# Calling square root and exponential once ahead of need, and splitting the wait for the first tokens

## The chip, the cores and the metric

The kernel runs on one core of a Trainium2 chip. The metric is the device time of one execution in microseconds; before the change it is 1632.89 us, the median of three runs (1627.72 to 1634.83). Lower is better.

## What is computed

One inference step of a hybrid backbone with two layers, in float32, on 128 context tokens and 256 latent tokens of 1024 channels:

```
for i in range(2):
    h = rms_norm(x, norm_mix[i]) * (1 + sc1) + sh1
    m = hyena_mixer(h) if i == 0 else rglru_mixer(h)
    x = x + g1 * m
    h = rms_norm(x, norm_moe[i]) * (1 + sc2) + sh2
    x = x + g2 * moe_ffn(h)          # 16 experts, top 2 of the best group
y = rms_norm(x, norm_final)

# moe_ffn, for the tokens of expert e:
scores = softmax(h @ router_w)
y = (silu(xblk @ w1[e]) * (xblk @ w3[e])) @ w2[e]
```

There are five norms: norms 0 and 1 in layer 0, norms 2 and 3 in layer 1 (the code calls the index `tag`; odd ones stand before the experts), and the final one.

## The kernel before

Each engine has a program of its own, written out by hand, and semaphores tie them. `PER` holds, for each semaphore, how often it is raised in a layer; `before(name, l)` is the count before layer l, so that a wait can name a place in a layer.

**Norm.** x lies with the channels on the partitions, in eight tiles of 384 tokens. ScalarE squares each tile as VectorE finishes it (`squares`, L519), TensorE sums over channels by a multiplication with ones, and ScalarE takes the root of 96 columns (`norm_root`, L531). VectorE takes the reciprocal, TensorE spreads it over the partitions, VectorE multiplies (L1366), and ScalarE (five tiles, L540) and VectorE (three) modulate.

**Router.** TensorE computes the logits, ScalarE copies them out (L756), and TensorE transposes them. VectorE reduces, finds the maximum and subtracts it (L1683); ScalarE takes the exponential (L759); VectorE picks groups, experts and gates in a long row of small instructions. Meanwhile ScalarE copies the normed tokens out of PSUM (`token_tile`, L752). ScalarE's table of functions is loaded where an instruction needs another one than is loaded (ACT_TABLE_LOAD in the trace, under the line of the instruction); these loads aren't written in the code.

**Experts.** An expert layer takes the 16 experts two at a time, eight rounds of a loop. For a pair, `tokens_of_two` gathers 64 tokens for each expert, transposed, by multiplying the tokens `h` with one-hot matrices `pick`: the channels 0 to 511 into PSUM bank 0, then 512 to 1023 into bank 6 (`TOKEN_BANKS`). ScalarE copies both banks to `xT` (L764 ahead of the loop, L574 in it). For each expert TensorE then multiplies with w1 (channels 0 to 511 first, then the rest), w3 and w2. The gather for the next pair lies in the second half of a round, between the w3 matrix and the w2 matrix of the pair's second expert. Experts with more than 64 tokens get extra passes of 32. Outputs are combined one expert later and added to x by VectorE (L1774).

**Weights.** SyncE loads 2 MB pieces into eight buffers, six pieces an expert. Those of the first expert and two pieces of the second are loaded ahead; the next wait in the queue (L369, L370) until TensorE has given a buffer back.

The copy ahead of the loop and TensorE's wait for it:

```
act.wait_ge(S("xT_mm"), before("xT_mm", l) + 1)
for i, bank in enumerate(TOKEN_BANKS):
    last = a.activation(xT[:, i, :, :], PS[:, bank, :]..., ACT.Copy)
last.then_inc(S("xT"), 1)
...
pe.wait_ge(S("xT"), before("xT", l) + group + 1)
```

Of the kernel before, what the change touches and what calls it, by code (L numbers as in the profile page):

```python
# [12 lines left out]
ACT = mybir.ActivationFunctionType  # L13
AX = mybir.AxisListType.X

P = 128
# [96 lines left out]
class Chain:  # L113
# [5 lines left out]
    def link(self, instruction):  # L119
# [5 lines left out]

PER = dict(sq=8, ss_mm=1, rms=1, rinv=1, rb_mm=1, nrm=8, hT_act=BY_ACT, hT_dve=KD - BY_ACT, ada_mm=12, o_mm=8, x_upd=8,
           rt_mm=3, rt_ev=1, rt_exp=1, rt_max=1, rt_mask=1, tok_mm=6, tok=6, route=1, pick=18, gpick=17,
           xT_mm=8, xT=8, w1_mm=16, w13_mm=16, sig=16, hid=16, gpT_mm=16, gpT=16, hidT_mm=16, hidT=16, w2_mm=16, yo=16,
           c_mm=128, acc_done=128)
def before(name, index):  # L130

    return PER[name] * index
# [100 lines left out]
def program(nc, A, y_prompt, y_sample, new_state):  # L233
    where, (pool, pool_order, pool_count) = plan(), pool_plan()
    with ExitStack() as ctx:
# [5 lines left out]
        def S(name):  # L241
            if name not in sems:
                sems[name] = ctx.enter_context(nc.semaphore(name))
            return sems[name]
# [20 lines left out]
        small = sb("small", [P, 100])  # L265
        PS = ctx.enter_context(nc.psum_tensor("PS", [P, 8, HALF], F32))
# [17 lines left out]
        eps = small[:, 81:82]  # L284
# [46 lines left out]
        xT = cut(hT, 576, 2 * HALF).rearrange("p (i c m) -> p i c m", i=2, m=P)  # L331
        gpT = cut(hT, 1600, N)
        hid = cut(hT, 1984, HALF)
# [153 lines left out]
        def _(act):  # L487
# [27 lines left out]
            def squares(tag, ks, sem=None, value=0):  # L515
                for n, k in enumerate(ks):
                    if sem is not None:
                        act.wait_ge(S(sem), value + n)
                    a.activation(h_ch[:, k, :], xc[:, k, :], ACT.Square).then_inc(S("sq"), 1)  # L519
# [13 lines left out]
            def modulate(tag):  # L533
# [3 lines left out]
                for k in range(BY_ACT):  # L537
# [3 lines left out]
                                           bias=MOD[:, l, 8 * sh + k, s:s + 1], scale=MODA[:, tag, k, s:s + 1])  # L541
                    ins.then_inc(S("hT_act"), 1)

            def norm(tag, sem, value):
                squares(tag, NORM_ORDER[tag], sem, value)
                norm_root(tag)
                modulate(tag)

            def expert_layer(l):
                with act.Fori(0, NE // UNROLL) as group:  # L550
                    for r in range(UNROLL):
                        e = group * UNROLL + r
                        extra = act.value_load(counts_i[0:1, bass.ds(e, 1)], min_val=0, max_val=NX)
                        done = act.value_load(counts_i[0:1, NE:][0:1, bass.ds(e, 1)], min_val=0, max_val=2 * LAYERS * NX)
                        act.wait_ge(S("w1_mm"), before("w1_mm", l) + e + 1)
                        a.activation(hid, PS[:, 2, :], ACT.Sigmoid).then_inc(S("sig"), 1)  # L556
                        with act.If(extra > 0):
                            with act.Fori(0, extra) as j:
                                n = done + j
                                act.wait_ge(S("x_gpT_mm"), n + 1)  # L560
                                a.activation(XgpT, PS[:, 7, 0:N], ACT.Copy).then_inc(S("x_gpT"), 1)
                                act.wait_ge(S("x_xT_mm"), n + 1)
                                a.activation(XxT, PS[:, 1, 0:256].rearrange("p (c m) -> p c m", m=P), ACT.Copy) \
                                    .then_inc(S("x_xT"), 1)
                                act.wait_ge(S("x_w1_mm"), X_BEGUN + n + 1)
                                a.activation(Xhid, PS[:, 4, 0:256], ACT.Sigmoid).then_inc(S("x_sig"), 1)
                                act.wait_ge(S("x_hT_mm"), n + 1)
                                a.activation(XhidT, PS[:, 0, 0:256].rearrange("p (c m) -> p c m", m=P), ACT.Copy) \
                                    .then_inc(S("x_hT"), 1)
                        if r:  # L570
                            with act.If(group < NE // UNROLL - 1):
                                act.wait_ge(S("xT_mm"), before("xT_mm", l) + group + 2)
                                for i, bank in enumerate(TOKEN_BANKS):
                                    last = a.activation(xT[:, i, :, :], PS[:, bank, :].rearrange("p (c m) -> p c m", m=P), ACT.Copy)  # L574
                                last.then_inc(S("xT"), 1)
                        act.wait_ge(S("hidT_mm"), before("hidT_mm", l) + e + 1)
                        a.activation(hidT, PS[:, 2, :].rearrange("p (c m) -> p c m", m=P), ACT.Copy) \  # L577
                            .then_inc(S("hidT"), 1)
                        act.wait_ge(S("gpT_mm"), before("gpT_mm", l) + e + 1)
                        act.wait_ge(S("c_mm"), SPREAD + before("c_mm", l) + 8 * e)  # L580
                        a.activation(gpT, PS[:, 3, 0:N], ACT.Copy).then_inc(S("gpT"), 1)
# [155 lines left out]
            for l in range(LAYERS):  # L737

                if l == 0:
                    mixer0()  # L740
                else:
                    norm(2, "acc_done", ADDED + before("acc_done", l) - 7)
                    mixer1()

                norm(2 * l + 1, "x_upd", 8 * l + 1)
                if l:
                    act.dma_start(nf, A["norm_final"].partition_broadcast(P)).then_inc(S("nf_in"), 16)

                def token_tile(i):
                    act.wait_ge(S("tok_mm"), before("tok_mm", l) + i + 1)  # L750

                    a.activation(h[:, i // 2, i % 2 * HALF:i % 2 * HALF + HALF].rearrange("p (k c) -> p k c", k=4),  # L752
                                 PS[:, 2 + i, :].rearrange("p (c k) -> p k c", k=4), ACT.Copy).then_inc(S("tok"), 1)

                act.wait_ge(S("rt_mm"), before("rt_mm", l) + 1)
                a.activation(pre[:, 0, :], PS[:, 0, 0:N], ACT.Copy).then_inc(S("rt_ev"), 1)  # L756
                token_tile(0)
                act.wait_ge(S("rt_max"), before("rt_max", l) + 1)
                a.activation(rt(0), rt(0), ACT.Exp).then_inc(S("rt_exp"), 1)  # L759
                for i in range(1, 6):  # L760
                    token_tile(i)
                act.wait_ge(S("xT_mm"), before("xT_mm", l) + 1)
                for i, bank in enumerate(TOKEN_BANKS):
                    last = a.activation(xT[:, i, :, :], PS[:, bank, :].rearrange("p (c m) -> p c m", m=P), ACT.Copy)  # L764
                last.then_inc(S("xT"), 1)
                act.wait_ge(S("route"), before("route", l) + 1)
                expert_layer(l)

            for i in range(6):  # L770
                act.wait_ge(S("y_mm"), i + 1)
                a.activation(hT[:, HALF * i:HALF * i + HALF], PS[:, 2 + i, :], ACT.Square, accum_out=sumsq[:, i:i + 1]) \
                    .then_inc(S("y_sq"), 1)
# [13 lines left out]
        def _(pe):  # L787
# [323 lines left out]
            def tokens_of_two():  # L1111
                for i, bank in enumerate(TOKEN_BANKS):
                    for c in range(4):
                        at = HALF * i + P * c
                        for t in range(NT):
                            last = mm(PS[:, bank, P * c:P * c + P], h[:, t, at:at + P], pick[:, t, :], t == 0, t == NT - 1)
                last.then_inc(S("xT_mm"), 1)

            def weight(r, c):
                return ring[:, moe_slot(r, c), :].rearrange("p (k n) -> p k n", k=4)  # L1120
# [1 line left out]
            def expert_layer(l):  # L1122
# [80 lines left out]
                with pe.Fori(0, NE // UNROLL) as group:  # L1203
                    for r in range(UNROLL):
                        e = group * UNROLL + r
                        extra = pe.value_load(counts_i[0:1, bass.ds(e, 1)], min_val=0, max_val=NX)
                        done = pe.value_load(counts_i[0:1, NE:][0:1, bass.ds(e, 1)], min_val=0, max_val=2 * LAYERS * NX)
                        pe.wait_ge(S("xT"), before("xT", l) + group + 1)
                        for b, at, done_sem in ((2, 0, "w1_mm"), (3, 2, "w13_mm")):
                            for k in range(KD):  # L1210
                                half = k // 4
                                c = at + half
                                if k % 4 == 0:
                                    arrived(c, r, group)
                                for g in range(2):
                                    last = mm(PS[m * g:m * g + m, b, :], xT[:, half, k % 4, m * r:m * r + m],
                                              weight(r, c)[:, k % 4, HALF * g:HALF * g + HALF], k == 0, k == KD - 1)
                            last.then_inc(S(done_sem), 1)
# [71 lines left out]
        def _(dve):  # L1290
# [465 lines left out]
            def expert_layer(l):  # L1756
# [64 lines left out]
                with dve.Fori(0, NE // UNROLL) as group:  # L1821
                    for r in range(UNROLL):
# [9 lines left out]
                        ch.link(take(pcols, rankm, e + 2))  # L1832
                        ch.link(v.tensor_scalar(xcols[:, 0:3], xcols[:, 0:3], -float(BASE), None, ALU.add))
                        extra_picks()
                        dve.wait_ge(S("xT_mm"), before("xT_mm", l) + group + 1)
                        one_hot(pick[:, :, BASE * r:BASE * r + BASE], base_iota, pcols, None, BASE, "pick")

                        dve.wait_ge(S("sig"), before("sig", l) + e + 1)
# [99 lines left out]
```

## Time and profile before

| what | value |
|---|---|
| median of three runs | 1632.89 us |
| the profiled execution's own time | 1633.03 us |
| its span, first to last instruction | 1631.2 us |
| TensorE busy | 1519.3 us, 93% of the span |
| VectorE busy | 688.6 us, 42% |
| ScalarE busy | 311.4 us, 19% |
| mean granted clock of TensorE | 0.976 of full speed |
| moved by DMA | 495.70 MB, mean 304 GB/s |

Busy shares are averages over stages with different limits; what ends a wait is read from the stage itself. A granted clock of 1.00 is 2.4 GHz and 0.50 is 1.2 GHz.

### The profile page before, as it was taken

The numbers are of one execution on the slowest core, as the hardware profiler recorded it, in microseconds if no ns is written. First come the engines' busy times: TensorE is split into PE (matmuls) and PEld (weight loads), VectorE is DVE, ScalarE is ACT, GpSimd is POOL, SyncE is SP. The second block draws the span as 40 slices with busy tenths as digits, with TensorE's granted clock in tenths as the row PEclk, the third lists the DMA queues.
The fourth block names the chain that finished last, engine by engine and source line by source line (L and its number), as shares of the span: only waits on it lengthen the run. The fifth ranks groups of instructions, "written<-read, shape, count | busy, mean of one in ns | idle before, by whom it ended". The sixth has DMA issues, their size and how long they took to land.

```text
span 1631.2 us, 22649 instructions
## 1 busy us (share of the span) xinstructions
PE 1519.3 (93%) x8134; PEld 734.2 (45%) x8135; DVE 688.6 (42%) x2059; ACT 311.4 (19%) x521; POOL 0.2 (0%) x4
## 2 busy tenths in 40 slices
PE   6999999997799999999999799897999998999996
PEld 3454555654344444344343455454344434344432
DVE  3334666433334434343343648835143343343344
ACT  4332222131010111010010347513110001011001
POOL 0000000000000000000000000000000000000000
PEclk9999999998999999999999899997999999999998
DMA  9438767750777999999979601524599997999994
GB/s 342 151 104 306 259 258 258 289 236 17 321 298 305 416 426 428 424 426 428 424 324 409 206 1 52 206 103 168 229 421 424 426 429 337 412 428 424 427 428 182
DMA packets 67568, 495.70 MB, mean 304 GB/s; under 512 B 4464, under 2 KB 21120, under 8 KB 28224
## 3 DMA queue, kind: packets, MB, share of 16 engines
q1 hardware_dynamic: 66048, 489.33, 73.5%
q10 hardware_dynamic: 1472, 5.72, 1.1%
q8 instruction: 32, 0.52, 0.1%
q14 instruction: 16, 0.13, 0.0%
HBM read 493.45 MB, written 1.58 MB: 303 GB/s over the span
## 4 chain that ended last, share of the span: by engine, by line
PE 80%; DMA 10%; DVE 5%; ACT 2%; issue 2%; SPq 0%; DVEq 0%; ACTq 0%
PE PS L789 77%; DMA halves<-in_moe_w 9%; PE PS L793 3%; DMA halves<-in_ada_w 1%; DVE xc L1774 1%; DVE halves L1597 0%; DVE misc L1597 0%; DVE halves L1588 0%; DVE halves L1590 0%; DVE halves L1589 0%; ACT hT L540 0%; ACT halves L694 0%; ACT L759 0%; ACT L531 0%; ACT L699 0%
## 5 line engine op out<-in xcount | busy, mean ns | idle before, releaser
L789 PE MATMUL PS<-halves,hT 128*64 128x512 f32 x3072 | 671.5, 595 | 19.7 <-DMA halves<-in_moe_w 16.6
L789 PEld LDWEIGHTS PS<-halves,hT 128*64 128x64 f32 x3072 | 216.8, 137 | 462.3 <-issue 430.2
L1774 DVE SCALAR_TENSOR_TENSOR xc<-PS,MOD,xc 128x128 f32<-128x128 f32 x592 | 196.0, 410 | 92.2 <-PE PS L789 90.8
L789 PE MATMUL PS<-hT,halves 128*128 128x384 f32 x640 | 219.8, 499 | 8.4 <-ACT halves L660 6.5
L789 PEld LDWEIGHTS PS<-hT,halves 128*128 128x128 f32 x640 | 122.0, 194 | 107.3 <-issue 23.9
L789 PE MATMUL PS<-halves 128*128 128x384 f32 (+1 forms) x336 | 118.5, 512 | 0.7 <-ACT pre L607 0.7
L789 PE MATMUL PS<-hT,misc 64*128 64x384 f32 x512 | 105.7, 521 | 4.1 <-DVE xc L1774 2.4
L789 PE MATMUL PS<-stack,h 128*128 128x128 f32 x768 | 96.7, 290 | 12.5 <-issue 5.2
L1841 DVE TENSOR_TENSOR hT<-hT,PS 128x512 f32<-128x512 f32 x32 | 22.0, 688 | 196.4 <-PE PS L789 196.4
L789 PEld LDWEIGHTS PS<-stack,h 128*128 128x128 f32 x768 | 93.7, 204 | 23.7 <-issue 19.5
L556 ACT ACTIVATE hT<-PS 128x512 f32<-128x512 f32 x32 | 19.1, 597 | 384.5 <-PE PS L789 384.5
L789 PEld LDWEIGHTS PS<-halves 128*128 128x128 f32 x336 | 63.4, 190 | 53.9 <-issue 17.1
L1853 DVE COPY misc<-PS 128x512 f32<-128x512 f32 x32 | 22.1, 692 | 142.4 <-PE PS L789 75.2
L1839 DVE TENSOR_TENSOR hT<-hT,PS 128x512 f32<-128x512 f32 x32 | 22.0, 688 | 112.5 <-ACT hT L556 112.5
L789 PEld LDWEIGHTS PS<-hT,misc 64*128 64x128 f32 x512 | 50.4, 190 | 41.6 <-issue 12.3
L577 ACT ACTIVATE hT<-PS 128x512 f32<-128x512 f32 x32 | 19.1, 597 | 178.0 <-PE PS L793 178.0
L574 ACT ACTIVATE hT<-PS 128x512 f32<-128x512 f32 x28 | 15.2, 595 | 184.2 <-PE PS L789 184.2
L1393 DVE SCALAR_TENSOR_TENSOR h<-pre,VT,h 128x127 f32<-128x127 f32 (+1 forms) x80 | 29.6, 412 | 45.8 <-ACT h L611 28.6
L793 PE MATMUL PS<-cst,hT 128*128 128x128 f32 x272 | 42.1, 299 | 5.0 <-DVE xc L1774 4.1
L789 PE MATMUL PS<-halves,cT 128*32 128x512 f32 x384 | 46.0, 598 | 0.7 <-DMA halves<-in_ada_w 0.7
L607 ACT ACTIVATE pre<-PS,VT 128x384 f32<-128x384 f32 x24 | 14.0, 581 | 165.1 <-PE PS L789 165.1
L793 PEld LDWEIGHTS PS<-cst,hT 128*128 128x128 f32 x272 | 33.3, 177 | 25.3 <-issue 18.9
(233 smaller groups left out, 1065.5 us busy)
## 6 DMA issues: line engine op xcount, KB each, us to landing
halves<-in_moe_w SPq DMA_DIRECT2D x192, 2048.0 KB, 17.6
halves<-in_ada_w SPq DMA_DIRECT2D x48, 1024.0 KB, 6.5
halves<-in_hy_w_in SPq DMA_DIRECT2D x12, 1024.0 KB, 5.1
halves<-in_rg_w_in SPq DMA_DIRECT2D x4, 2048.0 KB, 15.8
halves<-in_hy_w_out SPq DMA_DIRECT2D x4, 1024.0 KB, 8.1
halves<-in_rg_w_out SPq DMA_DIRECT2D x2, 2048.0 KB, 10.1
halves<-in_rg_wa SPq DMA_DIRECT2D x1, 2048.0 KB, 13.2
halves<-in_rg_wx SPq DMA_DIRECT2D x1, 2048.0 KB, 15.5
```

Source lines behind the costliest of these rows:

```text
L556: a.activation(hid, PS[:, 2, :], ACT.Sigmoid).then_inc(S("sig"), 1)
L574: last = a.activation(xT[:, i, :, :], PS[:, bank, :].rearrange("p (c m) -> p c m", m=P), ACT.Copy)
L577: a.activation(hidT, PS[:, 2, :].rearrange("p (c m) -> p c m", m=P), ACT.Copy) \
L607: a.activation(pre[:, ct % 2, :], PS[:, ct % 2, 0:N], ACT.Identity, bias=VT[:, 0, HB + ct:HB + ct + 1]).then_inc(S("in_ev0"), 1)
L789: return nc.tensor.matmul(out, lhsT, rhs, start=start, stop=stop)
L793: return nc.tensor.transpose(out, in_, ident[0:n, 0:n])
L1393: last = v.scalar_tensor_tensor(o, i, weight, o, ALU.mult, ALU.add)
L1774: ins = v.scalar_tensor_tensor(xc[:, k, cs], PS[:, bank, cs], MOD[:, l, 8 * G2 + k, s:s + 1], xc[:, k, cs], ALU.mult, ALU.add)
L1839: ch.link(v.tensor_tensor(hid, hid, PS[:, 2, :], ALU.mult))
L1841: v.tensor_tensor(hid, hid, PS[:, 3, :], ALU.mult).then_inc(S("hid"), 1)
L1853: v.tensor_copy(yo, PS[:, 6, :]).then_inc(S("yo"), 1)
```

## The change

A helper `table(function)` is added. It calls a function on the constant `eps`, one column, into an unused column of `small`, so that the table is loaded there. It is called with square root ahead of the squares of norms 1, 2 and 3 and of the final norm, and with exponential after the modulation of norms 1 and 3, ahead of the copy of the logits.

The gather raises its semaphore once for each bank instead of once for both. ScalarE waits for each bank and raises `xT` for each half. TensorE waits for a half of the tokens right before the first w1 matmul that reads it, and only at a pair's first expert. VectorE's wait counts both banks.

```
-           xT_mm=8, xT=8, ...
+           xT_mm=16, xT=16, ...

+            def table(function):
+
+                a.activation(small[:, 99:100], eps, function).then_inc(S("table"), 1)
+
             def norm(tag, sem, value):
+                if tag:
+                    table(ACT.Sqrt)
                 squares(tag, NORM_ORDER[tag], sem, value)
...
                         if r:
                             with act.If(group < NE // UNROLL - 1):
-                                act.wait_ge(S("xT_mm"), before("xT_mm", l) + group + 2)
                                 for i, bank in enumerate(TOKEN_BANKS):
-                                    last = a.activation(xT[:, i, :, :], PS[:, bank, :].rearrange("p (c m) -> p c m", m=P), ACT.Copy)
-                                last.then_inc(S("xT"), 1)
+                                    act.wait_ge(S("xT_mm"), before("xT_mm", l) + 2 * group + i + 3)
+                                    a.activation(xT[:, i, :, :], PS[:, bank, :].rearrange("p (c m) -> p c m", m=P), ACT.Copy) \
+                                        .then_inc(S("xT"), 1)
...
+                table(ACT.Exp)
                 act.wait_ge(S("rt_mm"), before("rt_mm", l) + 1)
                 a.activation(pre[:, 0, :], PS[:, 0, 0:N], ACT.Copy).then_inc(S("rt_ev"), 1)
...
-                act.wait_ge(S("xT_mm"), before("xT_mm", l) + 1)
                 for i, bank in enumerate(TOKEN_BANKS):
-                    last = a.activation(xT[:, i, :, :], PS[:, bank, :].rearrange("p (c m) -> p c m", m=P), ACT.Copy)
-                last.then_inc(S("xT"), 1)
+                    act.wait_ge(S("xT_mm"), before("xT_mm", l) + i + 1)
+                    a.activation(xT[:, i, :, :], PS[:, bank, :].rearrange("p (c m) -> p c m", m=P), ACT.Copy) \
+                        .then_inc(S("xT"), 1)
...
+            table(ACT.Sqrt)
             for i in range(6):
                 act.wait_ge(S("y_mm"), i + 1)
...
                         for t in range(NT):
                             last = mm(PS[:, bank, P * c:P * c + P], h[:, t, at:at + P], pick[:, t, :], t == 0, t == NT - 1)
-                last.then_inc(S("xT_mm"), 1)
+                    last.then_inc(S("xT_mm"), 1)
...
-                        pe.wait_ge(S("xT"), before("xT", l) + group + 1)
                         for b, at, done_sem in ((2, 0, "w1_mm"), (3, 2, "w13_mm")):
                             for k in range(KD):
...
                                 if k % 4 == 0:
+                                    if b == 2 and r == 0:
+                                        pe.wait_ge(S("xT"), before("xT", l) + 2 * group + half + 1)
                                     arrived(c, r, group)
...
-                        dve.wait_ge(S("xT_mm"), before("xT_mm", l) + group + 1)
+                        dve.wait_ge(S("xT_mm"), before("xT_mm", l) + 2 * group + 2)
```

## Rows read from the trace of the kernel before

**Rows 1.** The page: the chain that ended last, by engine.

```profile
PE 80%; DMA 10%; DVE 5%; ACT 2%; issue 2%; SPq 0%; DVEq 0%; ACTq 0%
```

**Rows 2.** Stretches: us, busy of PE, PEld, DVE, ACT, POOL, granted clock, DMA share, GB/s.

```profile
640.00:700.00 60.00, 57.39 (x303) 25.05 (x301) 21.33 (x74) 5.74 (x9) 0.00 (x0) 1.00 1.01 427
...
934.00:938.00 4.00, 4.00 (x7) 2.04 (x7) 3.69 (x13) 3.98 (x8) 0.00 (x0) 0.50 0.01 4
938.00:942.00 4.00, 4.00 (x12) 2.31 (x11) 2.84 (x17) 0.74 (x3) 0.00 (x0) 0.87 0.00 0
```

**Rows 3.** Groups by line, ScalarE: busy us, mean ns, idle before.

```profile
L531 ACT ACT_TABLE_LOAD x3 | 3.8, 1283 | 0.1
```

**Rows 4.** Timeline, norms 1 and 3: start us, us, instruction, idle before and releaser.

```profile
353.02 0.52 ACT L519 ACTIVATE h<-xc 128x384 f32<-128x384 f32 x1 [2.06 <-DVE xc L1665]
354.04 0.34 ACT L531 ACTIVATE rs<-PS,small 128x96 f32<-128x96 f32 x1 [0.49 <-PE PS L789]
...
1112.02 0.52 ACT L519 ACTIVATE h<-xc 128x384 f32<-128x384 f32 x1 [4.64 <-DVE xc L1665]
1112.56 1.28 ACT L531 ACT_TABLE_LOAD   x1
1113.85 0.34 ACT L531 ACTIVATE rs<-PS,small 128x96 f32<-128x96 f32 x1
```

**Rows 5.** The chain in order of time, norm 2: start us, us, what.

```profile
926.65 0.52 ACT h L519
...
928.49 0.35 ACT rs L531
```

**Rows 6.** Timeline, the end: variance and root.

```profile
1622.72 0.17 DVE L1871 TENSOR_SCALAR small<-small 128x3 f32<-128x3 f32 x1
...
1623.80 0.21 ACT L775 ACTIVATE small<-small 128x3 f32<-128x3 f32 x1
```

**Rows 7.** Timeline, ScalarE before norm 2 and before the final norm.

```profile
922.10 5.07 ACT L519 ACTIVATE h<-xc 128x384 f32<-128x384 f32 x8 [9.13 <-DVE xc L1774]
...
1617.98 0.60 ACT L772 ACTIVATE hT<-PS 128x512 f32<-128x512 f32 x1 [14.36 <-PE PS L793]
```

**Rows 8.** Timeline, the router in layer 0 and in layer 1.

```profile
357.11 4.49 ACT L540 ACTIVATE hT<-hT,MOD,MODA 128x128 f32<-128x128 f32 x10 [2.73 <-DVE hT L1366]
...
362.97 0.49 ACT L756 ACTIVATE pre<-PS 128x384 f32<-128x384 f32 x1 [1.37 <-PE PS L789]
...
364.80 0.21 DVE L1683 TENSOR_TENSOR misc<-misc 128x48 f32<-128x48 f32 x1
...
365.46 0.24 ACT L759 ACTIVATE misc<-misc 128x48 f32<-128x48 f32 x1
...
1119.07 2.34 ACT L540 ACTIVATE hT<-hT,MOD,MODA 128x256 f32<-128x256 f32 x5
...
1123.39 0.49 ACT L756 ACTIVATE pre<-PS 128x384 f32<-128x384 f32 x1 [1.99 <-PE PS L789]
...
1125.22 0.21 DVE L1683 TENSOR_TENSOR misc<-misc 128x48 f32<-128x48 f32 x1
...
1125.90 0.24 ACT L759 ACTIVATE misc<-misc 128x48 f32<-128x48 f32 x1
```

**Rows 9.** Timeline, gather, copies and first matrix, layer 0; first matrices, layer 1.

```profile
375.93 7.18 PE L789 MATMUL PS<-stack,h 128*128 128x128 f32 x48 [2.14 <-DVE stack L1766]
...
384.36 12.23 PE L789 MATMUL PS<-halves,hT 128*64 128x512 f32 x55 [1.26 <-ACT hT L764]
...
1145.15 13.96 PE L789 MATMUL PS<-halves,hT 128*64 128x512 f32 x64 [1.25 <-ACT hT L764]
```

**Rows 10.** Line L1207, TensorE's queue at loop entry: ns, first and last start.

```profile
L1207 PEldq SEQ_ASSERT  x1: 18/18/18, 382.8 to 382.8; - x1
```

**Rows 11.** Timeline, TensorE's weight loads behind a branch in the expert loop.

```profile
556.43 0.95 PEld L789 LDWEIGHTS PS<-hT,misc 64*128 64x128 f32 x8 [0.81 <-issue]
```

**Rows 12.** Waits of SyncE's queue, 364 to 415 us: total, times, longest.

```profile
SPq L369 <- PE PS L789: 18.4, 1, 18.4
```

More of the change, by code:

```diff
@@ L127 @@
            rt_mm=3, rt_ev=1, rt_exp=1, rt_max=1, rt_mask=1, tok_mm=6, tok=6, route=1, pick=18, gpick=17,
-           xT_mm=8, xT=8, w1_mm=16, w13_mm=16, sig=16, hid=16, gpT_mm=16, gpT=16, hidT_mm=16, hidT=16, w2_mm=16, yo=16,
+           xT_mm=16, xT=16, w1_mm=16, w13_mm=16, sig=16, hid=16, gpT_mm=16, gpT=16, hidT_mm=16, hidT=16, w2_mm=16, yo=16,
            c_mm=128, acc_done=128)
```

## Prediction

> **What bounds the kernel now.** I read the chain that ended last first. It stands on TensorE for 80% of the span and on weight transfers for 10%; ScalarE holds 2% [rows 1]. So anything that only shortens ScalarE can give little, and only at the places where TensorE stands still for it. Next the stretches: inside an expert layer, once it is under way, the DMA share is 1.01 and TensorE is busy 57.39 of 60 us, so there the weight stream sets the pace [rows 2]. Both changes lie outside those stretches: at the norms, in the router, at the first expert of each layer and at the end. The question is what each place gives and whether it passes through to the end.
>
 The timeline of the roots [rows 4] shows what matters most here: the load doesn't wait for what the root waits for. At norm 3 the last square ends at 1112.02 + 0.52 = 1112.54, the load starts at 1112.56, the root at 1113.85. The load runs while TensorE still sums the squares.
>
> **The change part by part.** *Roots of norms 2 and 3.* From the start of the last square to the root: 1.02 us without a load (354.04 - 353.02), 1.83 with one at norm 3 (1113.85 - 1112.02) [rows 4], 1.84 at norm 2 (928.49 - 926.65) [rows 5]. Hoisting gives 0.82 + 0.81 = 1.63 us, not two full loads. The hoisted load and call (1.29 from load to next instruction [rows 4] and 0.21, the length of a three-column call [rows 6]) stand before squares that wait for VectorE, 9.13 us at norm 2 [rows 7]; at norms 1 and 3 they wait for the residual in the same way. Without that cover each would cost 1.50 us.
>
> *Exponential of the router, twice.* VectorE's subtraction ends at 364.80 + 0.21 = 365.01, the exponential starts at 365.46 behind its load [rows 8]. With 0.02 us for the handoff it could start at 365.03: 0.43 us gained. In layer 1: 1125.45 against 1125.90, 0.45 us. The hoisted call stands ahead of the copy of the logits, and behind that copy are queued the first token tile and, through TensorE's transposes, VectorE's whole routing. In layer 0 modulation ends at 357.11 + 4.49 = 361.60; 1.29 and 0.21 later it is 363.10, and the copy starts at 362.97 now: up to 0.13 late. In layer 1: 1119.07 + 2.34 + 1.50 = 1122.91, before 1123.39, free. Net 0.30 + 0.45 = 0.75 us (bounds 0.7 and 0.9, if the short call overlaps the copy).
>
> The rows put 0.02 us between the square's end and the load, and 1.29 from there to the root [rows 4]. The Trainium skill (ScalarE: Activation LUTs, What ACT_TABLE_LOAD costs) counts 1.28 us for the load and some 1.38 of drain, 2.66 together. By that rule the copy of the logits would be late by about 1.5 and 0.9 us and the whole sum would be an estimated 3.4 us. The rows have no place for a drain after a short wait, so I go by 1.29.
>
> *Final root.* VectorE's variance is ready at 1622.72 + 0.17 = 1622.89; the root starts at 1623.80 [rows 6]. 0.89 us. The load moves into a wait of 14.36 us [rows 7]. Behind the root only the reciprocal, three scalings and the output transfers follow, each started by the one before, so all of it counts.
>
> *Tokens of the first pair, once per layer.* The gather takes 7.18 us from 375.93, to 383.11. Then ScalarE copies both halves, and TensorE starts the first matrix at 384.36 after 1.26 us of idle time (1.25 in layer 1) [rows 9]. Afterwards the first half's copy runs at about 375.93 + 3.59 = 379.5, under the second half of the gather. The second copy takes about half of the 1.26 us and ends near 383.8. It is wanted only after 16 matmul instructions of 13.96 / 64 = 0.218 us, 3.5 us after 383.1, so it is covered. The first matrix can start as the gather ends. What could come up in place of the wait is the loop's entry: reading two counters into registers. It is over at 382.8, before the gather's last matmul [rows 10]. I take 1.2 us per layer, 2.4 in all; upper bound 1.25 each, lower bound 0.4 each, if starting the loop's block costs TensorE what a branch in the expert loop does, 0.81 us put down to issue [rows 11].
>
> *In the loop* the same split costs and gives nothing: the fourteen pairs of copies run under the combines of the previous expert, far ahead of the next first matrix. TensorE, ScalarE and VectorE have the same number of waits or one more, and the wait of VectorE means the same moment. The cover is those combines and the second matrices; without it a group would gain what the first pair does.
>
> *Does it pass through?* The stream of weights starts anew only when expert 0 gives its buffers back: SyncE waits 18.4 us for TensorE there after the router [rows 12]. So the saturated stretch moves with TensorE's start, and in the mixer and the norms no row shows TensorE waiting for a weight. I pass everything on one to one.
>
> Sum: 1.63 + 0.75 + 0.89 + 2.4 = 5.67 us. The profiled execution took 1633.03 us (span 1631.2 and 1.8 around it), 0.14 above the median of the runs, so 1627.4 and, against the median, 1627.2 us: 0.35% faster. That lies within what a measurement of this kernel can tell from no change, about 0.5% or 8.2 us; the three runs alone spread over 7.1.
>
> **Rivals.** *(a) The split gives little*, since the loop's entry takes the place of the wait. For it: this row is from a queue that waited anyway. Against: it ended before the gather [rows 10]. 5.67 - 1.6 = 4.1 us, 1628.8. Chance 0.07.
>
> *(b) The weight stream swallows what lies ahead of an expert layer*, if its stretch is bound from transfers begun before the router. Only norm 2 and the final root remain, 0.82 + 0.89 = 1.7 us: 1631.2. Against it stands the restart [rows 12]. Chance 0.06.
>
> *(c) TensorE's clock falls better.* The dense matmuls behind norm 2 run at a granted 0.50 (1.2 GHz) and come back to 2.4 within the next 4 us [rows 2]; before that TensorE had been mostly idle through the norm. Half of the busy 4.00 and 0.13 of the next 4.00 are lost there, 2.5 us. A shorter idle time ahead of it may save that, and some 1 us elsewhere: 1632.9 - 5.7 - 3.5 = 1623.7. Chance 0.12.
>
> *(d) The clock falls worse: slower than before.* The moved starts bring low clock to stretches that now run at 2.4 GHz. Each costs what norm 2's does, 2.5 us; it decides from 5.67 us on, that is 11.3 us of dense matmuls moved to 1.2 GHz, three such stretches. With four, 1632.9 - 5.7 + 10 = 1637.2. For it: the mean clock is 0.976, so low stretches exist. Against: the idle times only get shorter. Chance 0.04.
>
> *(e) The exponential or root still loads*, because the loads are placed otherwise than I think and the added calls bring loads without taking any away: 5.67 - 3.27 = 2.4 gained, minus nothing where hidden, 1630.5. Chance 0.03.
>
> **How the numbers follow.** The forecast has 0.68. Its own range is 1625 to 1629.5 by the bounds of the terms (4.0 to 6.0 us) and the scatter of a median. (a) and (e) lie in or beside it. For 8 in 10 I reach to (c) below and (b) above: 1622.8 to 1631.8. Faster by over 0.5% means below 1624.7: most of (c) and the forecast's lower tail, 0.14. Slower by over 0.5% is above 1641, only the far part of (d) and a shift between measurements: 0.02. The rest 0.84.
>
> **What would show it.** Load and root: no load between the last square and the root at norms 2 and 3, and 1.0 us between their starts. Router: the exponential right after VectorE's subtraction, the copy of the logits at most 0.15 us later than now after the modulation. First pair: TensorE's first matrix within 0.1 us of the gather's end. End: the root at VectorE's heels. Wrong: if the wait for the first half is replaced by idle time put down to issue, if TensorE waits more for weights in the expert layers by what the earlier start gave, or if the stretches behind the norms have another granted clock; that last would move the total by more than any single term.

## Result and the profile after

The kernel is 4.3% slower, and the forecast of 0.35% faster was wrong.

| | median | lowest to highest | runs |
|---|---|---|---|
| before | 1631.06 us | 1627.72 to 1634.83 | 4 |
| after | 1700.4 us | 1698.77 to 1703.22 | 4 |

The ratio is 1.0431, with a 95% interval of 1.0412 to 1.045. The profiled execution after took 1698.77 us, with a span of 1697.0; before the span was 1631.2.

The page of the changed kernel comes first: span, instruction queue (packets, MB, share of the DMA engines), the chain by engine and the expert matmuls (busy us, mean ns | idle before them, and what ended most of it).

```profile
span 1697.0 us, 22645 instructions
...
q8 instruction: 95, 1.56, 0.4%
...
PE 82%; DMA 6%; issue 6%; DVE 5%; ACT 2%; SPq 0%; DVEq 0%; ACTq 0%
...
L797 PE MATMUL PS<-halves,hT 128*64 128x512 f32 x3072 | 688.1, 606 | 63.6 <-issue 54.0
```

The same of the kernel before:

```profile
q8 instruction: 32, 0.52, 0.1%
...
L789 PE MATMUL PS<-halves,hT 128*64 128x512 f32 x3072 | 671.5, 595 | 19.7 <-DMA halves<-in_moe_w 16.6
```

In the chain, issue rose from 2% to 6% and DMA fell from 10% to 6% [rows 1]. The expert matmuls stood idle for 63.6 us instead of 19.7, mostly with nothing to wait for that the profile shows. The queue that brings instructions moved 95 packets instead of 32, each 16 KB.

The waits of TensorE's matmuls after (line waited for: us, times, longest) and then before:

```profile
PE PS L797 <- issue: 71.6, 15, 9.6
PE PS L797 <- DMA halves<-in_moe_w: 9.2, 8, 1.2
```

```profile
PE PS L789 <- DMA halves<-in_moe_w: 16.6, 15, 1.3
PE PS L789 <- issue: 5.2, 2, 3.2
```

Fourteen of the fifteen waits, 69.0 us, lie behind 1140 us, in the expert loop of layer 1. The timeline of TensorE shows where (start, us, instruction, idle before it and what ended it):

```profile
1176.60 5.62 PE L797 MATMUL PS<-stack,h 128*128 128x128 f32 x48 [2.27 <-issue]
...
1202.79 15.37 PE L797 MATMUL PS<-halves,hT 128*64 128x512 f32 x64 [9.56 <-issue]
...
1244.92 5.62 PE L797 MATMUL PS<-stack,h 128*128 128x128 f32 x48 [2.03 <-issue]
1269.25 16.27 PE L797 MATMUL PS<-halves,hT 128*64 128x512 f32 x64 [7.71 <-issue]
1312.80 5.62 PE L797 MATMUL PS<-stack,h 128*128 128x128 f32 x48 [2.54 <-issue]
1337.10 16.48 PE L797 MATMUL PS<-halves,hT 128*64 128x512 f32 x64 [7.68 <-issue]
```

A period is a round of the loop. Ahead of the 64 matmuls with which the second to the eighth round begin, TensorE stands 6.5 to 9.6 us, and in most rounds 2.0 to 2.6 us more ahead of the gather in its middle. Layer 0 runs the same loop body without this.

### The profile page after: what moved, and what is told of

It is laid out like the page before. It is cut to its first block, busy times and chain, and to the rows that moved or that the text cites. A ratio compares the mean times of both kernels' runs of the same rounds, so it can differ in the third digit from the quotient of the medians.

```text
span 1697.0 us, 22645 instructions
## 1 busy us (share of the span) xinstructions
PE 1532.3 (90%) x8134; PEld 735.9 (43%) x8135; DVE 688.5 (41%) x2059; ACT 314.2 (19%) x527; POOL 0.2 (0%) x4
## 4 chain that ended last, share of the span: by engine, by line
PE 82%; DMA 6%; issue 6%; DVE 5%; ACT 2%; SPq 0%; DVEq 0%; ACTq 0%
PE PS L797 79%; DMA halves<-in_moe_w 4%; PE PS L801 3%; DMA halves<-in_ada_w 1%; DVE xc L1783 1%; DVE misc L1606 0%; DVE halves L1606 0%; DVE halves L1597 0%; DVE halves L1599 0%; DVE halves L1598 0%; ACT hT L540 0%; ACT halves L700 0%; ACT L705 0%; ACT halves L692 0%; DVE h L1885 0%
## 5 line engine op out<-in xcount | busy, mean ns | idle before, releaser
L797 PE MATMUL PS<-halves,hT 128*64 128x512 f32 x3072 | 688.1, 606 | 63.6 <-issue 54.0
L797 PEld LDWEIGHTS PS<-halves,hT 128*64 128x64 f32 x3072 | 221.0, 140 | 518.5 <-issue 500.1
```

Source lines behind the costliest of these rows:

```text
L797: return nc.tensor.matmul(out, lhsT, rhs, start=start, stop=stop)
```

## The theories

**A.** TensorE's instructions come in blocks of 256, one packet of 16 KB each. I counted the instructions in the compiled programs (a float32 matrix call is four: the trace has two loads and two matmuls for it). A loop over the experts has some 1608, six blocks and 72 more, so it touches seven blocks or eight by where it begins. The trace of the kernel before bears the count out: TensorE runs 627 instructions in a round of layer 1 without extra tokens and 1114 in one with a single extra pass, so with the passes of both experts the loop holds 627 + 2 x 487 = 1601 and what no round runs.

The split moves the code because a value that a wait compares with may have to be computed in a register by an instruction of its own. In layer 0's loop the traces show one such addition more a round for the tokens' wait and two fewer for the wait behind each expert's w3 matrix (`yo`). So layer 0's loop is one instruction shorter (626 in a plain round instead of 627), and layer 1's loop begins one earlier; its own plain rounds have 627 in both. Theory A says that it began at the first instruction of a block (0 behind its edge) and now begins at the last of the block ahead (255 behind), touches eight blocks, and is fetched anew in each round. Layer 0's loop begins 160 behind an edge in both kernels. The 63 packets more are nine for each of the seven rounds behind the first. The instruction queue in one of them, from 1268.22 to 1336.07 us after:

```profile
q8 instruction: 9, 0.15, 0.9%
```

These are the eight blocks touched and one more, which I take to be the one behind them. TensorE runs 627 instructions in that round, and the blocks that it jumps over (the passes for extra tokens) are fetched with the others.

**B.** The split itself costs it: TensorE waits at each half for ScalarE's copies, or the waits in the loop are dear.

**C.** The table calls do it, by another order of ScalarE's work. (The expectations below call this D; their C is an ordering between ScalarE's copies and TensorE, and foretells what B does.)

The Trainium skill (Runtime: NRT & Kernel Launch, Instruction fetch mechanics) describes such blocks of 256 instructions and 16 KiB, room for 2048 instructions on TensorE, and a window of two blocks outside of which a taken branch has to fetch. The blocks agree with the queue's packets, 0.52 MB / 32. The window doesn't: of 460 to 910 us, inside layer 0's loop of seven blocks, the trace after has no packet of this queue. The room fits the runs below: loops of seven blocks stay, and those for which nine packets a round come do not.

## The experiments

Ratios are to runs of the kernel before on the same chip. Its medians there are 1629.8 to 1631.7 us, so a difference between kernels of different tables, or from the changed kernel, carries some 2 us of that.

### One instruction more, one fewer, and each half alone

`e1_pad1` is the changed kernel with one needless wait of TensorE, on a semaphore that has long had its value, between the two expert loops:

```
                 else:
+                    pe.wait_ge(S("ones_in"), 16)
                     norm(2 * l)
```

> The changed kernel with one instruction more in TensorE's program, a wait for a semaphore reached long before, ahead of norm 2, so that the expert loop of layer 1 begins where it began before the change. Theory A (position of the code: in the changed kernel the loop of layer 1 spans one block of 16 KB more, and is fetched again in each of its rounds): the instruction queue moves 32 packets instead of 95, TensorE has no issue gaps at the loop's start, time 1624 to 1628 us. Rival B (the split wait itself, at the head of the loop, is what holds TensorE up): it stays at 1697 to 1703 us. Rival C (an ordering between ScalarE's copies and TensorE): the same as B.

`e2_minus1` is the kernel before with one wait fewer in layer 1, where it has long been met:

```
-                pe.wait_ge(S("rw_in"), 16)
+                if not l:
+                    pe.wait_ge(S("rw_in"), 16)
```

> The kernel before, with nothing of the change, but with one instruction less in TensorE's program ahead of the loop of layer 1: the second, needless wait for the router's weights is left out. Theory A: the instruction queue moves about 95 packets, TensorE stands still 7 to 9 us at the start of each round of layer 1, time 1695 to 1708 us. Rivals B and C: 1628 to 1634 us as before.

`e3_tables` is the kernel before with the table calls alone:

```
+                if tag:
+                    table(ACT.Sqrt)
...
+                table(ACT.Exp)
...
+            table(ACT.Sqrt)
```

> The kernel before with the calls of square root and exponential alone; TensorE's program is that of before. Theory A and the forecast's terms: 3.3 us less, more if the clock behind norm 2 falls better, so 1625 to 1629 us. Rival D (the calls bring the slowdown, as by a load that delays the routing): above 1635 us.

`e4_split` is the kernel before with the split alone:

```
+           xT_mm=16, xT=16, ...
...
+                                    if b == 2 and r == 0:
+                                        pe.wait_ge(S("xT"), before("xT", l) + 2 * group + half + 1)
```

> The kernel before with the split wait alone, no added calls. TensorE's program is that of the changed kernel, one instruction less ahead of the loop of layer 1. Theory A: about 1701 to 1706 us, 95 packets. Rival B: the same. Rival D: about 1628 us.

| kernel | median | ratio, 95% | instruction packets | issue waits of TensorE |
|---|---|---|---|---|
| before | 1629.84 | | 32 | 5.2 us, 2 |
| e1_pad1 | 1624.17 | 0.9971 [0.9959, 0.9983] | 32 | 5.0 us, 2 |
| e2_minus1 | 1707.36 | 1.0476 [1.0461, 1.0491] | 95 | 69.0 us, 15 |
| e3_tables | 1627.44 | 0.9985 [0.9975, 0.9996] | 32 | 5.2 us, 2 |
| e4_split | 1704.45 | 1.0451 [1.0436, 1.0466] | 95 | 71.7 us, 15 |

One instruction decides. Added to the changed kernel it takes away the 63 packets and 76 us (1700.4 to 1624.17); taken from the kernel before, with no part of the change in it, it brings the same 63 packets and 77.5 us. B fails on both, and C on e3_tables. e1_pad1 has the lowest median of this study.

The waits in the trace of e1_pad1, and then of e2_minus1:

```profile
PE PS L797 <- DMA halves<-in_moe_w: 16.9, 16, 1.3
PE PS L797 <- issue: 5.0, 2, 2.5
```

```profile
PE PS L789 <- issue: 69.0, 15, 8.1
```

The loop of layer 1 in a window, after and then in e1_pad1 (stretch, length, busy of PE, PEld, DVE, ACT, POOL with their instructions, granted clock, DMA share, GB/s):

```profile
1140.00:1660.00 520.00, 446.50 (x2376) 187.59 (x2374) 163.72 (x567) 44.76 (x71) 0.00 (x0) 0.93 0.87 356
```

```profile
1140.00:1590.00 450.00, 434.02 (x2394) 184.39 (x2390) 163.60 (x567) 44.77 (x71) 0.00 (x0) 1.00 0.96 406
```

The gaps cost twice. TensorE stands still, and the granted clock of the stretch is 0.93 instead of 1.00. Between e1_pad1 and the changed kernel the issue waits add 71.6 - 5.0 = 66.6 us, the 3072 expert matmuls at their lower clock add 688.1 - 672.1 = 16.0, and waits for weights give back 16.9 - 9.2 = 7.7, since the stream goes on while TensorE stands. The sum is 74.9 us; the spans differ by 74.8.

### Where the edges lie

If A is right, the starts of the loops decide and nothing else. Fillers early in TensorE's program move both loops. Each is a call with one column of output, into a place that nothing reads, and counts four instructions. They stand in e1_pad1:

```
             mm(PS[0:64, 1, 0:N], f_w1, features, True, True).then_inc(S("f_mm"), 1)
+            for _ in range(12):
+                mm(PS[0:64, 7, 0:1], f_w1, features[:, 0:1], True, True)
```

The number of calls is 12 in e5_fill48, 25 in e6_fill100, 46 in e7_fill184, 47 in e8_fill188, 52 in e10_fill208 and 64 in e11_fill256. Eight blocks are touched, by my count, from 185 behind an edge on (184 + 1608 = 7 x 256).

> The padded kernel of e1_pad1 with 12 small matmuls (one column, 64 partitions, into an unused bank; 48 instructions by the count of four to a float32 matmul) behind TensorE's first matmul. Theory A by counting: each expert loop is about 1608 instructions, 6 blocks of 256 and 72 more. It spans 7 blocks if it begins 0 to 184 instructions behind a block's edge, and 8 if 185 to 255 behind. Layer 1's begins at 0 in e1_pad1 (one less changed everything), layer 0's 3168 instructions earlier, so at 160. With 48 more: layer 0 at 208, refetched in every round, layer 1 at 48, not. So the issue gaps of 7 to 9 us stand in layer 0 and not in layer 1, time 1685 to 1710 us. Rival E (only layer 1's loop, or anything about the first instruction of its block): 1624 to 1630 us with no gaps.

> The same with 25 small matmuls, 100 instructions. Theory A: layer 0 at 260, that is 4, layer 1 at 100, neither refetched: 1624 to 1631 us, the matmuls themselves costing a few us at the start at most. Rival E (any shift from the lucky place is slow): 1690 us or more.

> The same with 46 small matmuls, 184 instructions. Theory A: layer 0 at 88, layer 1 at 184, its last instruction the last of the seventh block: 1625 to 1634 us, no gaps. If the count of the loop is off by a few instructions it is slow like the next kernel.

> The same with 47 small matmuls, 188 instructions, one matmul more than e7_fill184. Theory A: layer 1 at 188, eight blocks, refetched in every round: 1690 to 1710 us. Rival E: within 1 us of e7_fill184.

> As e8_fill188 with five small matmuls more, 208 instructions. e8_fill188 was not refetched though its loop ends 4 instructions into an eighth block by the count. Theory A, amended (the queue goes back to the first block in vain only when the block behind the eighth has been asked for, which takes more than 4 and at most 24 instructions into it, as in e5_fill48): layer 1's loop begins at 208 and ends 24 into the eighth block, so it is refetched, layer 0's at 112 is not. Gaps in every round of layer 1, fewer us than in the changed kernel, where the loop's first instruction is the last of its block and two blocks are fetched in turn at the start: total 1655 to 1690 us. Rival E (the place behind a block's edge has no such meaning in layer 1): within 3 us of e8_fill188, about 1635.

> The same with 64 small matmuls, 256 instructions, one whole block. Theory A: both loops stand to the blocks as in e1_pad1, 33 packets, no gaps in the rounds; the time is that of e8_fill188 and some 3 us for the matmuls at the start, 1633 to 1640 us. Rival E: refetched, like e10_fill208 or worse.

| kernel | layer 0 begins | layer 1 begins | median | ratio, 95% | packets |
|---|---|---|---|---|---|
| e6_fill100 | 4 | 100 | 1627.44 | 0.9984 [0.9969, 0.9999] | 32 |
| e7_fill184 | 88 | 184 | 1633.45 | 1.0021 [1.0007, 1.0034] | 33 |
| e8_fill188 | 92 | 188 | 1634.43 | 1.0025 [1.0011, 1.0038] | 33 |
| e11_fill256 | 160 | 0 | 1633.28 | 1.0009 [0.9995, 1.0024] | 33 |
| e5_fill48 | **208** | 48 | 1668.27 | 1.0237 [1.0188, 1.0286] | 95 |
| e10_fill208 | 112 | **208** | 1683.75 | 1.0314 [1.0285, 1.0343] | 96 |

e5_fill48 and e10_fill208 ran twice each. e5_fill48 moves the fault into layer 0, as theory A has it, but missed its expectation of 1685 to 1710 us with gaps of 7 to 9: it is 1668.27, with 1.2 to 2.3 us at the head of a round. The instruction queue of its trace from 460 to 910 us, within layer 0's loop, and the timeline of one of its rounds:

```profile
q8 instruction: 58, 0.95, 0.8%
```

```profile
528.61 8.26 PE L797 MATMUL PS<-stack,h 128*128 128x128 f32 x48 [3.38 <-issue]
...
549.09 3.64 PE L797 MATMUL PS<-halves,hT 128*64 128x512 f32 x15 [1.21 <-issue]
552.98 10.94 PE L797 MATMUL PS<-halves,hT 128*64 128x512 f32 x49 [0.26 <-issue]
...
565.85 1.67 PE L797 MATMUL PS<-hT,misc 64*128 64x384 f32 x8 [1.93 <-issue]
```

The gap behind the first 15 matmuls (30 instructions with their loads, and some for counters and waits) stands at a block's edge, since a loop that begins at 208 meets one after 48 instructions. In layer 1's loop, from 1230 to 1600 us, the queue moves one packet. e10_fill208 turns it round: one packet from 460 to 910 us and 43 from 1230 to 1560. Its waits, and two gaps of a round in layer 1:

```profile
PE PS L797 <- issue: 48.2, 22, 3.4
```

```profile
1187.16 5.62 PE L797 MATMUL PS<-stack,h 128*128 128x128 f32 x48 [2.34 <-issue]
...
1206.85 15.28 PE L797 MATMUL PS<-halves,hT 128*64 128x512 f32 x64 [3.06 <-issue]
```

At 208 the head of a round costs 0.9 to 3.1 us, at 255 it costs 6.5 to 9.6 and nothing between the first matmuls. The same nine packets a round so cost 44 to 50 us at 208 (1668.27 against e1_pad1's 1624.17, 1683.75 against e11_fill256's 1633.28) and 76 at 255. A loop that begins with the last instruction of a block has to get that block and the next before its first matmul. The packets' times bear this out: in the trace after, one starts inside each of the seven gaps at a head, 5.5 to 6.5 us behind the one before it; in e5_fill48 and e10_fill208 none starts inside such a gap. e11_fill256, a whole block further than e1_pad1, is free again: the period is 256.

e8_fill188 missed its expectation. By my count it touches eight blocks, and it has 33 packets. The step from e7_fill184 to it is real. In the first round, which is fetched in any case, the gather is cut in the trace of e7_fill184 after 29 matmuls and in that of e8_fill188 after 27, two matmuls or four instructions earlier:

```profile
449.60 3.50 PE L797 MATMUL PS<-stack,h 128*128 128x128 f32 x29 [2.35 <-issue]
455.81 3.84 PE L797 MATMUL PS<-stack,h 128*128 128x128 f32 x19 [2.72 <-issue]
```

```profile
452.97 3.27 PE L797 MATMUL PS<-stack,h 128*128 128x128 f32 x27 [2.44 <-issue]
458.53 4.13 PE L797 MATMUL PS<-stack,h 128*128 128x128 f32 x21 [2.29 <-issue]
```

So the edge is where the count has it, but refetching begins somewhere from 4 to 24 instructions into the eighth block. The packets give the sign that goes with it: in e7_fill184 and e8_fill188 the last of the 33 packets comes behind layer 1's loop (at 1606.9 and 1609.5 us), while each refetched loop has nine packets a round. Either the loop's last few are fewer than I count, or reaching the eighth block isn't enough and the one behind it must have been asked for. These runs don't tell which.

The ratios of e7_fill184, e8_fill188 and e11_fill256 stand some 0.4 to 0.5% above e1_pad1's and that of e6_fill100 0.1%. By the traces most of this lies at the start, where the fillers stand ahead of matmuls that others wait for: the first ones on `stack` start at 16.62 us in e1_pad1 and at 17.83, 22.64, 22.73 and 26.46 in e6, e7, e8 and e11, and layer 0's loop begins at 381.0 and at 384.3, 386.3, 389.6 and 390.4. From there to the end all five take 1240 to 1245 us.

### The split alone, without the fault

`e9_split_pad` is e4_split with the wait of e1_pad1. It asks what the split is worth by itself.

> The split wait alone, without the added calls, and one instruction more in TensorE's program so that layer 1's loop begins where it does before the change. Theory A and the forecast's term: 32 packets, no gaps in the rounds, 2.4 us less than before, 1626 to 1629 us. Rival B (the split costs something in the loop of its own): above 1630 us, each round of both layers longer.

Its median is 1626.78 us against 1631.73 of the kernel before, a ratio of 0.9974 [0.9958, 0.999], with 32 packets. The gain is 4.95 us, and the interval spans 1.6 to 6.9, so the 2.4 of the forecast lies in it. Rival B of its expectation, a split that costs something by itself, is out: it asked for more than 1630 us. Whether the split brings more than its two waits, this run doesn't settle.

## Why the prediction was wrong, by its own steps

**The step that failed** stands in two sentences: "In the loop the same split costs and gives nothing", and of the loop's entry, "What could come up in place of the wait is the loop's entry: reading two counters into registers". I counted the waits that TensorE has in the loop, one more or as many, and asked what each would wait for. I didn't count the instructions, nor ask where the loops lie in TensorE's program. Both sentences hold for layer 0 and for e1_pad1; in layer 1 the entry and the gather cost 68.5 of the 69.0 us of issue, in rounds that the forecast had at nothing. The prediction's list of signs did name idle time put down to issue, but only in place of the first wait. No rival held it either. (d) had a lower clock in layer 1's loop, but by moved starts of dense stretches and at 2.5 us each; the clock there is 0.93 with the gaps and 1.00 in e1_pad1 without them. (a) had issue in place of the wait, at 1.6 us.

**The rest of the sum was right** but for the exponential of layer 0. Rows of the trace after, ScalarE and the final root (start, us, instruction):

```profile
361.35 1.28 ACT L546 ACT_TABLE_LOAD   x1
362.64 0.20 ACT L546 ACTIVATE small<-small 128x1 f32<-128x1 f32 x1
363.04 0.49 ACT L763 ACTIVATE pre<-PS 128x384 f32<-128x384 f32 x1 [0.20 <-PE PS L797]
...
365.11 0.24 ACT L766 ACTIVATE misc<-misc 128x48 f32<-128x48 f32 x1 [0.89 <-DVE misc L1692]
...
919.12 5.07 ACT L519 ACTIVATE h<-xc 128x384 f32<-128x384 f32 x8 [7.62 <-DVE xc L1783]
924.68 0.34 ACT L531 ACTIVATE rs<-PS,small 128x96 f32<-128x96 f32 x1 [0.49 <-PE PS L797]
...
1106.26 0.52 ACT L519 ACTIVATE h<-xc 128x384 f32<-128x384 f32 x1 [4.64 <-DVE xc L1674]
1107.28 0.34 ACT L531 ACTIVATE rs<-PS,small 128x96 f32<-128x96 f32 x1 [0.49 <-PE PS L797]
...
1689.35 0.17 DVE L1880 TENSOR_SCALAR small<-small 128x3 f32<-128x3 f32 x1
1689.56 0.21 ACT L783 ACTIVATE small<-small 128x3 f32<-128x3 f32 x1 [0.43 <-DVE small L1880]
```

- *Roots of norms 2 and 3*, forecast 0.82 + 0.81. At norm 3 the root starts 1.02 us after the last square, at norm 2 0.49 after the end of the squares (919.12 + 5.07 = 924.19; 1.32 before, [rows 5, 7]): 0.81 and 0.83.
- *Exponential*, forecast 0.30 + 0.45. From the modulation (356.84 after, 357.11 before [rows 8]) to the exponential it is 8.27 us against 8.35: only 0.08. The copy of the logits came 6.20 us after the modulation's start instead of 5.86, so 0.34 late, not 0.13: I had set the call's end as the copy's start, and it starts 0.40 us behind the call's beginning (362.64 and 363.04). In layer 1 it gave 0.43 (6.40 us from the modulation's last row to the exponential, 6.83 before [rows 8]), and the copy wasn't late. Together 0.51 of 0.75.
- *No drain*: 1.29 us from load to the call, as before [rows 4]. By the 2.66 us that the Trainium skill counts for a switch (ScalarE: Activation LUTs, What ACT_TABLE_LOAD costs) the call would have started at 364.01, behind the copy that in fact began at 363.04. The trace doesn't agree with it here.
- *Final root*, forecast 0.89: 0.21 us behind VectorE's start instead of 1.08 [rows 6], so 0.87.
- *First pair*, forecast 1.2 per layer. The gather ends at 375.58 + 7.54 = 383.12, and the first matrix runs on from it with no idle time, while the second copy starts at 383.15. The same holds in layer 1, so the waits of 1.26 and 1.25 us [rows 9] are gone:

```profile
375.58 7.54 PE L797 MATMUL PS<-stack,h 128*128 128x128 f32 x48 [2.15 <-DVE stack L1775]
...
380.47 0.60 ACT L771 ACTIVATE hT<-PS 128x512 f32<-128x512 f32 x1 [12.69 <-PE PS L797]
...
383.05 13.95 PE L797 MATMUL PS<-halves,hT 128*64 128x512 f32 x64
383.15 0.60 ACT L771 ACTIVATE hT<-PS 128x512 f32<-128x512 f32 x1 [2.08 <-PE PS L797]
```

- *Does it pass through?* In e1_pad1, yes: 1629.84 - 1624.17 = 5.67 us, the sum of the forecast, though the ratio's interval is 2.8 to 6.7 us, which makes so close a match luck. e3_tables alone gave 2.4 of a forecast 3.3. Rival (b), the stream swallowing it, would have left 1.7, just outside.
- *Rival (c)* isn't borne out. In the trace after, TensorE's return to 2.4 GHz behind norm 2 comes earlier; in e1_pad1, with the same change, the low clock lasts as long as before, 10.2 us against 6.8 after. After and then e1_pad1 (stretch, length, busy times, clock):

```profile
929.00:933.00 4.00, 3.23 (x6) 1.91 (x7) 4.00 (x12) 4.00 (x10) 0.00 (x0) 0.55 0.36 114
933.00:937.00 4.00, 4.00 (x14) 2.34 (x13) 2.73 (x16) 2.02 (x4) 0.00 (x0) 1.00 0.00 0
```

```profile
925.00:929.00 4.00, 2.11 (x6) 1.28 (x5) 3.45 (x8) 2.79 (x7) 0.00 (x0) 0.50 0.91 288
929.00:933.00 4.00, 4.00 (x9) 2.19 (x9) 3.04 (x13) 3.19 (x6) 0.00 (x0) 0.67 0.01 5
```

Before it is 0.50 up to 938 [rows 2]. ScalarE's first copy of layer 1's mixer starts at 936.62 instead of 941.72, 5.1 us sooner, but 3.0 of this is there when the squares of norm 2 begin (919.12 and 922.10). From the squares to that copy it is 19.62 us before, 17.50 after and 18.41 in e1_pad1, of which the root explains 0.83. The rest is no more than the traces differ without the change: from layer 0's last expert to layer 1's first, by the reads of their counters, it is 272.9 us before and 269.0 after, but also 270.0 in e2_minus1, which has nothing of the change. For the same reason the 5.67 us of e1_pad1 can't be divided among the terms by its trace.

## What to carry to other kernels

A change that adds or removes a single instruction ahead of a long loop can cost more than all that it was made for: count the instructions of TensorE's loops, note how many blocks of 256 they touch, and after any edit compare the instruction queue's packets and the issue waits with those of before. If the packets jump, one needless wait ahead of the loop moves it back; by the limit seen here a loop of up to six blocks (1536 instructions) would not depend on its place, since it touches seven at most. That is an estimate; no run here has such a loop. A good reading of the waits can be right in every term and the time still wrong, so undo parts and pad before blaming the change.

## What the hardware showed that was not expected

- TensorE's loop of about 1608 instructions runs from what it holds when it begins 0 to 188 instructions behind an edge (0, 4, 48, 88, 92, 100, 112, 160, 184 and 188 were seen), and is fetched in each round at 208 (e5_fill48 and e10_fill208) and 255. Past the limit it isn't the one block too many that comes anew but all of them, nine packets a round, though a plain round runs only 627 of the instructions.
- The gaps of refetching lie where the weight stream takes all of the DMA engines. Around the first gap, the queues from 1195 to 1203 us after (packets, MB, share):

```profile
q1 hardware_dynamic: 423, 3.38, 101.3%
q8 instruction: 1, 0.02, 0.8%
```

One block of 16 KB comes in these 8 us, and its packet takes 1.0 us of them (0.8% of 16 engines). The packets of this queue take 1.05 us in the mean after and 1.03 before, so the gap isn't their own length. What fills the rest, and whether the stream holds the fetch up, wasn't tested.
- A table is loaded 1.28 us ahead of the instruction that needs it, also while the engine would wait for that instruction's operand, so hoisting a call gained 0.81 to 0.87 us at the roots, 0.43 and 0.08 at the exponentials, and nowhere the whole load.
